# Expert weights in six transfers of 1 MB, or in three of 2 MB with 16 KB per partition

## The reference

```python
def expert_block(args):                      # D_MODEL 1024, D_EXPERT 512
    xb, e = args                             # 128 rows of tokens, one expert of 32
    h = jax.nn.silu(xb @ w1[e]) * (xb @ w3[e])
    return h @ w2[e]
...
out = lax.map(expert_block, (xs.reshape(nb, MOE_BLOCK, D), block_e)).reshape(nb * MOE_BLOCK, D)
g_sorted = gates.reshape(-1)[order].astype(x2d.dtype)
return jax.ops.segment_sum(out[dest] * g_sorted[:, None], tok, num_segments=T)
```

## Time and profile before

| What | Value |
|---|---|
| median of 3 runs | 1024.66 us (1024.5 to 1025.6) |
| profiled execution, its own time | 1025.62 us |
| its span, first to last instruction | 1024.0 us |
| mean granted TensorE clock | 0.957 of full |
| PE busy | 921.0 us (90%) |
| PEld / DVE / POOL / ACT busy | 587.5 / 247.6 / 157.4 / 111.0 us |
| DMA packets | 57935, 258.22 MB |
| queue q1 (SP) | 47740 packets, 238.54 MB, 60.6% of 16 engines' span |
| queue q0 (POOL) | 10144 packets, 18.95 MB, 8.1% |
| loads of expert weights | 192 of 1024 KB, median 25.9 us from issue to landing |

### The profile page before, as it was taken

How to read it: one execution, slowest core, us unless ns; L and a number is a source line. 1 busy time by engine, 2 the same in 40 slices (tenths; PEclk the granted TensorE clock), 3 DMA queues, 4 the chain that set the end, 5 groups by cost and what they waited for, 6 DMA issues and landing times. The chain is left out here.

```text
span 1024.0 us, 24939 instructions
## 1 busy us (share of the span) xinstructions
PE 921.0 (90%) x10522; PEld 587.5 (57%) x10522; DVE 247.6 (24%) x760; ACT 111.0 (11%) x172; POOL 157.4 (15%) x239
## 2 busy tenths in 40 slices
PE   5999999999999973999999999989988999898940
PEld 2545545455455542876777677657556685674620
DVE  1434452454534553410000000000000000000006
ACT  0211110111101110001010101010010010010004
POOL 1000000000000002112222222212112122112110
PEclk9999999999999995999999999999989999998985
DMA  8760010100101063999999999999999999999938
GB/s 340 277 251 21 22 41 0 41 21 21 41 0 43 39 247 98 394 366 390 363 387 363 370 367 369 368 372 376 368 390 375 379 384 380 355 389 363 326 70 322
DMA packets 57935, 258.22 MB, mean 252 GB/s; under 512 B 11410, under 2 KB 12490, under 8 KB 40853
## 3 DMA queue, kind: packets, MB, share of 16 engines
q1 hardware_dynamic: 47740, 238.54, 60.6%
q0 software_dynamic: 10144, 18.95, 8.1%
HBM read 234.55 MB, written 24.60 MB: 253 GB/s over the span
## 5 line engine op out<-in xcount | busy, mean ns | idle before, releaser
L1186 PEld LDWEIGHTS ps<-hT,big 128*64 128x64 f32 x8192 | 286.4, 138 | 40.1 <-issue 28.6
L1186 PE MATMUL ps<-hT,big 128*64 128x64 f32 (+8 forms) x8192 | 294.7, 233 | 14.7 <-DMA big<-in_exp_w 7.9
L1202 PE MATMUL ps<-big,poolT 128*64 128x512 f32 (+8 forms) x512 | 233.8, 609 | 11.3 <-DMA big<-in_exp_w 7.5
L1083 PE MATMUL ps<-big,hT 128*128 128x512 f32 x384 | 169.9, 602 | 3.3 <-DMA big<-in_w_in 1.9
L1202 PEld LDWEIGHTS ps<-big,poolT 128*64 128x64 f32 (+8 forms) x512 | 75.1, 152 | 145.8 <-issue 135.2
L985 DVE TENSOR_TENSOR poolT<-u,ps 128x256 f32<-128x256 f32 (+8 forms) x32 | 15.1, 472 | 505.1 <-PE ps L1186 467.4
L1083 PEld LDWEIGHTS ps<-big,hT 128*128 128x128 f32 x384 | 73.2, 193 | 94.6 <-issue 88.5
L545 POOL DMA_INDIRECT x_rows<-xn,sidx x32 | 49.4, 1545 | 385.3 <-ACT xn L695 363.3
L695 ACT ACTIVATE xn<-ps,gslot 64x1024 f32<-64x1024 f32 (+8 forms) x32 | 35.5, 1110 | 456.0 <-PE ps L1202 240.8
L525 POOL DMA_INDIRECT slot_table<-ids,dest x18 | 18.7, 1038 | 328.2 <-DVE dest L807 271.9
L1140 PE MATMUL ps<-big,yT 128*128 128x512 f32 x128 | 56.4, 593 | 0.9 <-DVE yT L874 0.9
(11 more groups left out here) (168 smaller groups left out, 469.1 us busy)
## 6 DMA issues: line engine op xcount, KB each, us to landing
big<-in_exp_w SPq DMA_DIRECT2D x192, 1024.0 KB, 25.9
big<-in_w_in SPq DMA_DIRECT2D x4, 1536.0 KB, 13.5
big<-in_w_out SPq DMA_DIRECT2D x2, 2048.0 KB, 14.9
x_rows<-xres SPq DMA_DIRECT2D x8, 512.0 KB
h_rows<-xn SPq DMA_DIRECT2D x8, 512.0 KB, 2.7
big<-x_rows SPq DMA_DIRECT2D x8, 512.0 KB, 7.3
out_y_prompt<-big SPq DMA_DIRECT2D x8, 512.0 KB, 2.9
xres<-in_x_prompt SPq DMA_DIRECT2D x1, 3072.0 KB, 11.1
```

The lines of the kernel that those rows point to most:

```text
L1083: last = pe.matmul(ps[0:m, bank, :], hT[:, k, 0:m], win[:, k, part * AW:(part + 1) * AW], start=(k == 0), stop=(k == KD - 1))
L1186: last = pe.matmul(out[c * w:(c + 1) * w, j, 0:m], up_weights(n)[:, k, j * P + c * w:j * P + (c + 1) * w], xT[:, 4 * half + k, 0:m], start ...
L1202: last = pe.matmul(ps[0:m, 5 + cols, :], hhT[:, 2 * half + k, 0:m], down_weights(n)[:, k, cols * 512:(cols + 1) * 512], start=(half + k == ...
```

## The change

`CH` is 3 and `CHW` 4096: `big` has six buffers of 2 MB (16 KB per partition), three for each `s`, one for w1, one for w3, one for w2. A load is one whole matrix. For w2, partition p now holds rows 4p to 4p+3 (one run of 16 KB) in place of rows p, p+128, p+256, p+384 (four runs of 4 KB). The hidden units of w1 and w3 must come out in the same order, so that hidden unit 4p+j is on partition p of slice j: PE's stationary operand of slice j is now every fourth column (`up_columns`) in place of 64 neighbouring ones. A buffer is free, and a load visible, only as a whole.

```diff
-CH = 6
-CHW = 2048
+CH = 3
+CHW = 4096
...
             def chunk_src(e, c):
-                half = c % 2
-                if c < 4:
-                    w = (exp_w1, exp_w3)[c // 2]
-                    return w[0, e].rearrange("(p k) n -> p (k n)", k=KD)[:, half * CHW:(half + 1) * CHW]
-                return exp_w2[0, e, half * 2 * P:(half + 1) * 2 * P, :].rearrange("(k p) n -> p k n", p=P)
...
+                if c < 2:
+                    return (exp_w1, exp_w3)[c][0, e].rearrange("(p k) n -> p (k n)", k=KD)
+                return exp_w2[0, e].rearrange("(p k) n -> p (k n)", k=KF)
...
-            for n in range(10, 2 * CH):
-                sp.dma_start(chunk_dst(n, n - CH), chunk_src(FIRST + 1, n - CH)).then_inc(chunk_in[n], 16)
+            for n in range(2 * CH - 1, 2 * CH):
+                sp.dma_start(chunk[n], chunk_src(FIRST + 1, n - CH)).then_inc(chunk_in[n], 16)
...
-            for n in range(CH, 10):
+            for n in range(CH, 2 * CH - 1):
                 load_chunk(FIRST + 1, n)
...
-                    act.wait_ge(used, CH * b + 2)
+                    act.wait_ge(used, CH * b + 1)
...
-                    dve.wait_ge(used, CH * b + 4)
+                    dve.wait_ge(used, CH * b + 2)
...
+            def up_columns(n, k, j, first):
+
+                return up_weights(n)[:, k, :].rearrange("p (q j) -> p j q", j=KF)[:, j, first:first + P // SPLIT]
...
-                        for half in range(2):
-                            n = CH * s + 2 * part + half
-                            pe.wait_ge(chunk_in[n], 16 * h + 16)
...
-                                                         up_weights(n)[:, k, j * P + c * w:j * P + (c + 1) * w],
...
+                        n = CH * s + part
+                        pe.wait_ge(chunk_in[n], 16 * h + 16)
...
+                                                     up_columns(n, k, j, c * w),
...
-                    for half in range(2):
-                        n = CH * s + 4 + half
-                        pe.wait_ge(chunk_in[n], 16 * h + 16)
...
+                    n = CH * s + 2
+                    pe.wait_ge(chunk_in[n], 16 * h + 16)
```

More of the change, by code:

```diff
@@ L431, in _ @@
             for n in range(CH):
-                sp.dma_start(chunk_dst(n, n), chunk_src(FIRST, n)).then_inc(chunk_in[n], 16)
+                sp.dma_start(chunk[n], chunk_src(FIRST, n)).then_inc(chunk_in[n], 16)
             store_h2(LAST, NS)
@@ L437, in load_chunk @@
             def load_chunk(e, n):
-                sp.dma_start(chunk_dst(n, n % CH), chunk_src(e, n % CH)).then_inc(chunk_in[n], 16)
+                sp.dma_start(chunk[n], chunk_src(e, n % CH)).then_inc(chunk_in[n], 16)
             def load_weights(h):
@@ L473, in _ @@
                     for c in range(CH):
-                        sp.dma_start(chunk_dst(c, c), chunk_src(e, c)).then_inc(ov_w, 16)
+                        sp.dma_start(chunk[c], chunk_src(e, c)).then_inc(ov_w, 16)
             for s in range(2):
@@ L1178, in block_pair @@
                     for part, out in enumerate((up1, up3)):
-                        for half in range(2):
-                            n = CH * s + 2 * part + half
-                            pe.wait_ge(chunk_in[n], 16 * h + 16)
[L1182 to L1186, removed]
-                                                         up_weights(n)[:, k, j * P + c * w:j * P + (c + 1) * w],
-                                                         xT[:, 4 * half + k, 0:m], start=(half + k + j == 0),
-                                                         stop=(half + k == 4), skip_group_check=True)
-                            last.then_inc(used, 1)
+                        n = CH * s + part
+                        pe.wait_ge(chunk_in[n], 16 * h + 16)
+                        for k in range(KD):
+                            for j in range(KF):
+                                for c in range(SPLIT):
+                                    w = P // SPLIT
+                                    last = pe.matmul(out[c * w:(c + 1) * w, j, 0:m],
+                                                     up_columns(n, k, j, c * w),
+                                                     xT[:, k, 0:m], start=(k + j == 0),
+                                                     stop=(k == KD - 1), skip_group_check=True)
+                        last.then_inc(used, 1)
                     if not (final and s):
@@ L1196, in block_pair @@
                     pe.wait_ge(hhT_ready, b + 1)
-                    for half in range(2):
-                        n = CH * s + 4 + half
-                        pe.wait_ge(chunk_in[n], 16 * h + 16)
[L1200 to L1205, removed]
+                    n = CH * s + 2
+                    pe.wait_ge(chunk_in[n], 16 * h + 16)
+                    for k in range(KF):
+                        for cols in range(2):
+                            last = pe.matmul(ps[0:m, 5 + cols, :], hhT[:, k, 0:m],
+                                             down_weights(n)[:, k, cols * 512:(cols + 1) * 512],
+                                             start=(k == 0), stop=(k == KF - 1))
+                    last.then_inc(used, 1)
             pe.wait_ge(onehot_ready, 1)
@@ L1224, in _ @@
                         for k in range(KD):
-                            last = pe.matmul(ps[:, 2 + m, :], xT[:, k, :], up_weights(2 * m + k // 4)[:, k % 4, :],
+                            last = pe.matmul(ps[:, 2 + m, :], xT[:, k, :], up_weights(m)[:, k, :],
                                              start=(k == 0), stop=(k == KD - 1))
@@ L1229, in _ @@
                     for k in range(KF):
-                        last = pe.transpose(ps[:, 4, k * P:(k + 1) * P], hh[:, k * P:(k + 1) * P], ident[:, :])
+                        last = pe.transpose(ps[:, 4, k * P:(k + 1) * P],
+                                            hh[:, :].rearrange("t (q k) -> t k q", k=KF)[:, k, :], ident[:, :])
                     last.then_inc(ov_hT, 1)
@@ L1235, in _ @@
                             last = pe.matmul(ps[:, 5 + cols, :], hhT[:, k, :],
[L1236 removed]
+                                             down_weights(2)[:, k, cols * 512:(cols + 1) * 512],
                                              start=(k == 0), stop=(k == KF - 1))
```

3 lines of the change are left out of this document (removed).

## The result

The kernel with three 2 MB buffers takes 1195.31 us (1193.87 to 1196.38, 4 runs) against 1025.13 (1024.5 to 1027.37, 4 runs) of the kernel before: ratio 1.1655, interval 1.1632 to 1.1677. It is slower, as forecast, by 170 us where 105 were forecast, and outside the range. The mechanism that the forecast rested on is not what made it slow. The profiled execution took 1193.87 us, with a span of 1192.3.

What follows compares the result with a forecast made beforehand. The prediction took the DMA engines as full, PE as nearly full and POOL's gate loop as 2 us short of the bound. It summed 1024.7 + 58 + 57 = 1140, took 1130 us, range 1040 to 1185.

Steps and rivals of the forecast that it cites:

- D: PE's every-fourth-column weight reads and the coarser buffers: 0 us for the reads, at most +3.5 us for buffers, taken as 0.
- B: POOL's scatter and gate-gather loop, first 20 blocks: 16 KB weight packets hold it back, +58 us (bounds +18 to +92).
- C: The same loop in the last eleven distances, with deep rings at 68 and 76 rows: +57 us (bounds +20 to +85).
- Rival 3: PE's strided weight load costs 10 ns on 4096 pairs, +41 us, half of it hidden: 1045 us; chance 0.04.
- A: Weight loads on the DMA engines: same bytes in fewer packets, -10 us, if the DMA engines stay the bound.
- Rival 1: DMA engines stay the bound, longer packets don't hold back the software queue: 1018 us, faster; chance 0.12.
- Rival 2: Gaps in the weight queue shelter POOL's loop, every block at the DMA's pace of 18.7 us: 1063 us; chance 0.12.

## Why the prediction was right and wrong

**D, PE's weight loads: the step that failed.** "L1032's stationary operand is read with a step of 8 floats, L1094's without; both take 192 ns, so 0." The rows are right and compare two things at once, a transpose against a matmul; the one with the step is of the kind that doesn't pay for it (the kernel with transposes as matmuls). In place of 0 stands 502.9 - 294.7 = 208 us of PE's time, of which 168 show. No row of before had a strided matmul load to read the price from; the rule of the Trainium skill on 16-byte lines (SBUF — State Buffer, the paragraph on cachelines) spoke against the change, and it wasn't weighed. That the kernel came out slower, as forecast, is luck as far as the reason goes: B and C, for which it was forecast, add nothing that shows in it.

**Rival 3** named this mechanism, with a chance of 0.04 and a price of 10 ns on 4096 pairs. Only the size was off: a pair of halves went from 60 to 122 ns with 56 rows and from 84 (before, from 515.26 us, 254 records of 96 rows took 10.72 us) to 122, which over all blocks is 208 us and not 41; 168 of it show and not half. Its sign in the profile, L1186 of 56 rows over 7.7 us a block, came: 15.6. The other one, PE above 960 us with ACT let go by PE, came too: 1119. PE's timeline before, a block of 96 rows:

```profile
515.26 10.72 PE L1186 MATMUL ps<-hT,big 128*64 128x96 f32 x254
```

**B, the loop held back by longer packets.** Not seen in the changed kernel, where PE's 23.4 us a block leave room for both the supply and the loop; its gates land in 6.5 us in the median (before 8.8). In the kernel with neighbouring columns it is there, step by step: nearly equal counts (42 and 39), gates letting go of ACT (26 of 30), and PE waiting at w2, though only 12.1 us in 7 waits. Its size was 25.7 us, not 58, and inside the bounds of 18 to 92: 19.1 us a block, not 20.7. The gates landed in 11.6 us in the median, under the 12 to 13 forecast, and the DMA share from 425 to 785 us stayed at 0.99, where under 0.95 was forecast; which term of the 19.7 us loop was too large is not shown. The mechanism is shown by its removal: the early gates take 23.2 of the 25.7.

**C, the blocks of 68 and 76 rows.** +14.4 us in the kernel with neighbouring columns where 57 was forecast, below the lower bound of 20. The long loops came nearly as forecast, the ones between did not. L690 in that kernel:

```profile
825.58 1.11 ACT L690 ACTIVATE xn<-ps,gslot 68x1024 f32<-68x1024 f32 x1 [15.45 <-DMA gslot<-gate_rows,pidx]
854.00 1.11 ACT L690 ACTIVATE xn<-ps,gslot 80x1024 f32<-80x1024 f32 x1 [26.98 <-DMA gslot<-gate_rows,pidx]
864.68 1.11 ACT L690 ACTIVATE xn<-ps,gslot 68x1024 f32<-68x1024 f32 x1 [9.29 <-PE ps L1199]
890.21 1.11 ACT L690 ACTIVATE xn<-ps,gslot 80x1024 f32<-80x1024 f32 x1 [20.51 <-DMA gslot<-gate_rows,pidx]
```

Behind 68 rows it is 28.4 and 25.5 us (forecast 26 to 29), but between them 10.7: PE had its products ready and its weights loaded, and made up what the long loop had lost. The sum had 19.6 there, a loop with a full queue. Part of the 14.4 may be the granted clock, 0.90 from 785 to 955 us where the earlier trace rows has 0.95; L1199 took 244.8 us in the whole kernel where L1202 had 233.8. (The recorded terms of a long loop, 7.05 + 22 to 24 x 0.61 + 4 to 6 + 2.8, add up to 27.3 to 30.5 us, not 26 to 29.)

**A, fewer packets.** -10 was forecast only if the DMA engines stay the bound. Where they did (the kernel with neighbouring columns and early gates, share 1.01) the rate was 374 GB/s, no gain that the profile shows. The 2.5% read from single stretches of 1.6 to 6 us did not carry to the mixed traffic.

**Rival 1** (the DMA engines stay the bound, 1018) is refuted: even without the stride the layout costs 41 us. **Rival 2** (1063) came out within 3 us of the kernel without the stride, 1065.63, but not for the reason it gave, that every block runs at the DMA engines' own pace of 18.7 us: the first 20 took 19.1 each, and with the gates out of the way 17.9. As a forecast for this change it missed by the same 130 us.

The sum that would have hit: 1024.7 + 168 (PE at 23.4 us a block) + 0 for all else, since B and C run beside PE's work and are shorter.

## What to carry to other kernels

Before a matmul's stationary operand is read with a step, count the bytes between its elements: up to two floats were free here, four doubled the load, and a layout that makes a transfer neater cost 168 us on PE where 10 us were hoped for on the DMA engines. A price must be read from a row of the same kind of instruction, and by busy time over count: the mean of a record rose from 222 to 283 ns with 56 rows while its share of PE doubled. The loop that stood in the waits of the kernel before cost nothing while the DMA engines were full, and began to cost when the packets that it waits behind grew; issuing its small gathers ahead of the large scatter took most of that back.

## What the runs showed of the hardware

- A record of a matmul with 64 fp32 weight columns takes 61 to 62 ns at steps of 4 and 8 floats; at steps of 1 and 2 all 8192 records take 295 us, 36 ns each in the mean. A whole tile of 128 columns takes 112 ns at step 1 and 234 at step 4.
- Two half tiles (60 ns) beat one whole tile (112 ns) with 56 moving rows; undoing the split costs 130 us here.
- In strided loads of whole tiles the granted clock fell to the 1.2 GHz level while PE was busy, and a record took no longer for it; in those of half tiles it stayed at 1.00.
- A transpose with a strided operand (step of 8 floats, 141 ns) doesn't pay what a matmul pays for the step; as an fp32 matmul it is two records, each 1.8 times as long.
- Row counts that divide by 16, more rows in all, went with 380 GB/s of full DMA engines, where early gates alone had 376.
